# Product-key expert layer on Trainium2: tile order, row buffers, one-hot matrices and a scratch layout changed

## The chip, the cores and the metric

One core of one Trainium2 chip runs the whole program, two transformer blocks in one launch. The metric is the device time of one execution in microseconds (us). TensorE is PE here, VectorE DVE, ScalarE ACT, GpSimd POOL, and SyncE, which only issues DMAs, SP. All data is fp32; products that need full fp32 accuracy are made of three matmuls over a high and a low part of each operand (fp32r).

## The reference, cut to what matters

The change touches only the last stage, the expert layer at the end of the second block. For each of 512 tokens and 8 heads it finds the 16 best sums of two key scores out of 128 x 128 experts, and adds the outputs of these 128 experts, each one a vector of 1024 numbers in (`expert_down`) and one out (`expert_up`):

```python
v1, i1 = lax.top_k(sc[..., 0, :], PEER_TOPK)
v2, i2 = lax.top_k(sc[..., 1, :], PEER_TOPK)
cand = (v1[..., :, None] + v2[..., None, :]).reshape(b, s, PEER_HEADS, PEER_TOPK * PEER_TOPK)
cidx = (i1[..., :, None] * PEER_N_KEYS + i2[..., None, :]).reshape(b, s, PEER_HEADS, PEER_TOPK * PEER_TOPK)
top, pos = lax.top_k(cand, PEER_TOPK)
idx = jnp.take_along_axis(cidx, pos, axis=-1)
gate = jax.nn.softmax(top, axis=-1)
...
u = expert_down[ib]
act = jax.nn.gelu(jnp.einsum('bld,blhkd->blhk', hb, u), approximate=False)
coef = (gb * act.astype(F32)).astype(hb.dtype)
vv = expert_up[ib]
return jnp.einsum('blhk,blhkd->bld', coef, vv)
```

## The kernel before, in words

The 512 tokens are four tiles of 128. Tiles 0 to 2 (`DENSE` = 3) are computed densely: PE multiplies them with all 16384 experts, and a matrix G of gates, zero nearly everywhere, picks the chosen ones. Tile 3 is gathered: each of its tokens has its 128 rows of `expert_down` and then of `expert_up` fetched from HBM.

The stage (`peer_experts`, L2071) is a loop over 128 blocks. Each brings 1 MB of weights: `expert_down` in blocks 0 to 63, `expert_up` in blocks 64 to 127. SP loads them into a ring of three (L2145, L2150), ACT makes the high part (L2306, two halves), DVE the low part (L2355, two halves), PE multiplies (L264 to L266 in the first half, L2289 in the second). high and low have two buffers: ACT's high part of block q waits until PE has done block q-2, and DVE's low part waits for the high part.

Beside this stream every block carries small tasks, handed out at build time by `peer_plan` (L1907) from a budget per block. DVE does them in program order behind the two low parts of its block:

- `sel`: 24 pieces per tile that choose the experts (`Selection.piece`, L2003). Pieces 0 to 9 and 11 to 15 are maximum and index searches (L1991 to L1999), pieces 17, 18, 20 and 21 are tensor_tensor operations on 128x2048 elements (L2037, L2041). A tile's scores are loaded only after the tile before is done (L2156). `finish` makes its gates.
- `g`: a group of four tokens of a dense tile, 96 groups in all. DVE writes for each token two one-hot matrices of 128 x 128, eight tensor_scalar operations in all (L2376, L2378, the second one with the gate multiplied in); PE multiplies them into G of these tokens (`spread_group`, L2247, eight short matmuls), and ACT copies G out (L2330). Four buffers of one-hot matrices (`AB_RING`). SP stores G of 16 tokens to HBM (L2166, 24 stores of 1 MB) and loads it back by keys in the second half (L2178, one load of 1.5 MB for every four blocks).
- `dot`, `coef`, `acc`: the gathered tile. A row of 128x1024 (one expert for each token) is gathered by POOL with an indirect DMA (L2208) into a ring of eight buffers, DVE multiplies and sums it (L2384; 128 rows), and after `coef` 128 rows of `expert_up` are added into the result (L2395). Four of the eight buffers are the score and candidate buffers of the selection, so rows are gathered only once all four tiles are selected: dots begin in block 37.

POOL's program (L2214) is, block by block: in the second half the product of the dense activations (a_tile, gelu stored in the first half and loaded back, L2187) with G (L2221, tensor_tensor on 128x768), then the gathers whose buffer was freed in an earlier block. Behind the product come ACT's high part (L2346), DVE's low part (L2360) and PE.

The plan before, by blocks: 0 to 35 `sel`, with 2 or 3 groups each from block 12 on; 36 to 51 two groups, and three dots each from 37 on; 52 to 63 four dots each; 64 to 75 two or three dots; 77 to 119 two or three accs.

Of the kernel before, what the change touches and what calls it, by code (L numbers as in the profile page):

```python
# [23 lines left out]
P = 128  # L24
D = 1024
# [1864 lines left out]
ROW_RING = 8  # L1890
# [15 lines left out]

def peer_plan():  # L1907
# [9 lines left out]
    before = {"dot": ("sel", DENSE, last), "coef": ("dot", PEER_SLOTS - 1), "acc": ("coef", 0)}  # L1917
# [8 lines left out]

    for b in range(PEER_BLOCKS):
        budget, many = 5.5, 0
        if finish and placed_by(b - 2, ("sel", finish[0], last)):
            place(b, ("finish", finish.pop(0)))  # L1930
        while sel and budget > 0:
            i, n = sel[0]
            if i and n == 0 and not placed_by(b - 1, ("sel", i - 1, last)):
                break
            assert n < 11 or i == 0 or placed_by(b - 1, ("finish", i - 1))
            place(b, ("sel", *sel.pop(0)))
            budget -= SEL_COST[n]
# [7 lines left out]
        while rows and taken < (3 if many or b >= PAIRS else 4):  # L1945
# [10 lines left out]
class Selection:  # L1956
# [4 lines left out]
    def __init__(self, nc, io, st, sc, cand):  # L1961
# [14 lines left out]
        self.gates = st.sb("gates", [P, 2, PEER_SLOTS])  # L1976
        self.row_f = st.sb("row_f", [P, 2, PEER_SLOTS])
# [25 lines left out]
    def piece(self, i, n, turned):  # L2003
# [19 lines left out]
        elif n == 16:  # L2023
# [5 lines left out]
            else:  # L2029
                dve.wait_ge(turned, i)  # L2030
# [14 lines left out]
        else:  # L2045
            if i == DENSE:
# [11 lines left out]
    def finish(self, i, turned):  # L2058
        H, T, order, dve = PEER_HEADS, PEER_TOP, self.order, self.dve
        dve.wait_ge(self.exp_ready, i + 1)  # L2060
        if i >= 2:
            dve.wait_ge(turned, i - 1)
# [3 lines left out]
        order(dve.tensor_tensor(self.gates[:, i % 2, :].rearrange("p (h t) -> p h t", h=H), t,  # L2066
# [4 lines left out]
def peer_experts(nc, io, hn, hnT, h, ident, score_dram, a_dram, g_dram, out):  # L2071
# [12 lines left out]
    n_rows = 2 * PEER_SLOTS  # L2084
    with Stage(nc, "peer") as st:
# [23 lines left out]
        cand_rows = cand[:, :, :, :].rearrange("p h a b -> p (h a b)")  # L2109
        rows = [hn[:, 0, :], hn[:, 1, :], hn[:, 2, :], h[:, NT, :], sc[:, 0:D], sc[:, D:2 * D],  # L2110
                cand_rows[:, 0:D], cand_rows[:, D:2 * D]]
# [11 lines left out]
        idx_done, row_used, dots_gelu, coef_done = (  # L2123
            st.sem(x) for x in ("idx_done", "row_used", "dots_gelu", "coef_done"))
# [9 lines left out]
        with nc.Block() as block:  # L2134

            @block.sync
            def _(sp):
                sp.dma_start(select.iota[:, :], io["c_iota128"].partition_broadcast(P)).then_inc(select.iota_in, 16)
                sp.dma_start(sc[:, :], score_dram[0]).then_inc(select.sc_in, 16)
                for q in range(PEER_BLOCKS + 6):  # L2140
# [12 lines left out]
                    for i in range(1, NT):  # L2153
                        if at[("sel", i - 1, last_piece)] + 3 == q:
                            sp.wait_ge(select.selected, i)
                            sp.dma_start(sc[:, :], score_dram[i]).then_inc(select.sc_in, 16)  # L2156
# [5 lines left out]
                    for n in range(G_BATCHES):  # L2162
                        per = G_BATCH // G_TOK
                        if group_at[n * per + per - 1] + 4 == q:
                            sp.wait_ge(group_taken, (n + 1) * per)
                            sp.dma_start(g_dram[:, n, :, :].rearrange("p k t -> p (k t)"),  # L2166
                                         staged[:, n % 2, :, :].rearrange("p k t -> p (k t)")
                                         ).then_inc(staged_out[n % 2], 16)

                    for g in range(G_LOADS):  # L2170
                        if q == max(PAIRS - 1, PAIRS - 2 + 4 * g):
# [6 lines left out]
                            sp.dma_start(g_tile[:, g % 2, :, :, :], g_dram[:, :, g * G_KEYS:(g + 1) * G_KEYS, :]  # L2178
# [10 lines left out]
                sp.wait_ge(row_used, n_rows)  # L2189
                sp.dma_start(out[DENSE * P:NT * P, :], h[:, DENSE, :]).then_inc(stored, 16)  # L2190
# [6 lines left out]
            def _(pool):  # L2197
                def gather(n):
# [3 lines left out]
                    if n == 0:  # L2202
                        pool.wait_ge(select.selected, NT)
# [10 lines left out]
                for q in range(PEER_BLOCKS):  # L2214
                    b = q - PAIRS + 1
# [10 lines left out]
                    while done < n_rows and (row_at[done - ROW_RING] + 1 if done >= ROW_RING else  # L2226
                                             at[("sel", DENSE, last_piece)] + 1) <= q:
# [4 lines left out]
            def _(pe):  # L2232
                def turn(i):
                    pe.wait_ge(select.finished, i + 1)
                    if i >= 1:
                        pe.wait_ge(turn_taken, i)
                    for w, src in enumerate((select.picked[:, 0, :, :].rearrange("p h t -> p (h t)"),
                                             select.picked[:, 1, :, :].rearrange("p h t -> p (h t)"),
                                             select.gates[:, i % 2, :])):
# [11 lines left out]
                for q in range(PAIRS):  # L2251
                    tasks = [t for t in plan[q] if t[0] in ("finish", "g") and t[1] < DENSE]
# [4 lines left out]
                    for j in range(2):  # L2257
# [3 lines left out]
                        for k in range(KD):  # L2261
# [5 lines left out]
                            if k % 2 and tasks and not (j == 0 and k == 1):  # L2267
                                kind, i, *n = tasks.pop(0)
                                if kind == "finish":
                                    turn(i)  # L2270
# [27 lines left out]
            def _(act):  # L2298
                for q in range(PEER_BLOCKS + 2):
# [16 lines left out]
                    for task in (plan[q - 1] if 1 <= q <= PEER_BLOCKS else ()):  # L2316
                        if task[0] == "finish" and task[1] < DENSE:
                            i = task[1]
# [30 lines left out]
            def _(dve):  # L2349
                accumulated = 0  # L2350
                for q in range(PEER_BLOCKS):
# [10 lines left out]
                    for task in plan[q]:  # L2362
# [5 lines left out]
                        elif kind == "g":  # L2368
# [17 lines left out]
                        elif kind == "coef":  # L2386
                            dve.wait_ge(dots_gelu, 1)
                            dve.tensor_tensor(coef[:, :], dots[:, :], select.gates[:, DENSE % 2, :], ALU.mult
                                              ).then_inc(coef_done, 1)
                            dve.wait_ge(coef_done, 1)  # L2390
                        elif kind == "acc":
# [4 lines left out]
                                                     h[:, DENSE, :], ALU.mult, ALU.add).then_inc(row_used, 1)  # L2396
                for t in range(DENSE):
# [6 lines left out]
def second_block(nc, io, x, ident, out, dbg=None):  # L2404
# [4 lines left out]
    g_dram = nc.dram_tensor("scratch_g", [P, G_BATCHES, PEER_KEYS, G_BATCH], F32).ap()  # L2409
# [304 lines left out]
```

## Time and profile before

| | us |
|---|---|
| median of three runs | 5074.52 |
| lowest, highest | 5065.39, 5079.26 |
| the profiled execution | 5070.14 |
| its span, first to last instruction | 5068.4 |
| PE busy in it | 4175.7 (82%) |
| DVE busy | 3274.8 (65%) |
| ACT busy | 1977.1 (39%) |
| POOL busy | 620.0 (12%) |

The stage that is changed is the last quarter of the span, from 3735 us on. Busy times are sums over the whole program; what bounds this stage must be read in windows of it. Instructions of DVE overlap by some 0.1 us, so that the distance between two starts, not the duration, is what an instruction takes of the engine.

### The profile page before, as it was taken

To read this page: it belongs to the slowest core of one execution; us is meant where nothing else is said; L and a number is where in the kernel's file an instruction comes from. 1 tells how busy PE (TensorE), PEld (TensorE's weight loads), DVE (VectorE), ACT (ScalarE), POOL (GpSimd) and SP (SyncE) were. 2 spreads that over 40 slices of the span, in tenths; PEclk is the share of its full clock that TensorE was granted. 3 is DMA by queue.
4 is the path that set the end of the run, shared out by engine and by line. 5 is a ranking of instruction groups with operands and counts; after the bars stand their busy time and mean duration, and the time that the engine had idled before them with its cause. 6 is when DMAs were issued, how large, how long until landed. Compare 5 with 4: busy or idle time off the path is not lost. (4 is left out here: it accounts for less than half of the span.)

```text
span 5068.4 us, 60013 instructions
## 1 busy us (share of the span) xinstructions
PE 4175.7 (82%) x22904; PEld 3325.7 (66%) x22904; DVE 3274.8 (65%) x4709; ACT 1977.1 (39%) x2044; POOL 620.0 (12%) x391
## 2 busy tenths in 40 slices
PE   6674568999999999994946596778789889988889
PEld 6573355566556556553836576678679889966677
DVE  2335737888888888884275434423249999777776
ACT  2212206667676766663222122222223333322222
POOL 0000000000000000000000000000000014565774
PEclk8887679999999999997957767989889999999999
DMA  2020019999999999994211002122245559999996
GB/s 85 18 68 21 26 57 358 365 355 365 364 360 358 365 367 352 367 367 141 68 35 58 28 1 85 59 65 78 71 146 167 185 194 366 393 334 324 338 335 232
DMA packets 485002, 1054.27 MB, mean 208 GB/s; under 512 B 21634, under 2 KB 188290, under 8 KB 472392
## 3 DMA queue, kind: packets, MB, share of 16 engines
q1 hardware_dynamic: 444248, 908.46, 50.4%
q0 software_dynamic: 40560, 143.16, 7.9%
q8 instruction: 129, 2.11, 0.2%
q14 instruction: 65, 0.53, 0.0%
HBM read 986.23 MB, written 65.32 MB: 207 GB/s over the span
## 5 line engine op out<-in xcount | busy, mean ns | idle before, releaser
L1254 DVE TENSOR_TENSOR ffn_low<-ffn_raw,ffn_high 128x2048 fp32r<-128x2048 f32 (+1 forms) x576 | 1189.7, 2109 | 261.8 <-ACT ffn_high L1207 261.7
L1207 ACT CAST ffn_high<-ffn_raw 128x2048 fp32r<-128x2048 f32 (+1 forms) x576 | 986.9, 1765 | 418.2 <-DMA ffn_raw<-in_w_gate 145.7
L2306 ACT CAST peer_high<-peer_raw 128x1024 fp32r<-128x1024 f32 x256 | 256.3, 1049 | 542.8 <-PE peer_ps L266 294.1
L264 PE MATMUL peer_ps<-peerbuf_hnT_high,peer_high 128*128 128x384 f32 x1024 | 354.8, 347 | 21.4 <-ACT peer_high L2306 19.3
L2355 DVE TENSOR_TENSOR peer_low<-peer_raw,peer_high 128x1024 fp32r<-128x1024 f32 x256 | 311.1, 1256 | 93.1 <-ACT peer_high L2306 92.7
L265 PE MATMUL peer_ps<-peerbuf_hnT_high,peer_low 128*128 128x384 f32 x1024 | 346.0, 338 | 0.0
L266 PE MATMUL peer_ps<-peerbuf_hnT_low,peer_high 128*128 128x384 f32 x1024 | 345.9, 338 | 0.0
L2289 PE MATMUL peer_ps<-peer_high,peerbuf_hnT_high 128*128 128x512 f32 x768 | 249.7, 408 | 82.1 <-DVE peerbuf_hnT_low L2360 74.0
L264 PE MATMUL ffn_gate_p<-ffn_high,ffn_x_high 128*66 128x512 f32 (+1 forms) x768 | 290.0, 378 | 19.9 <-DVE ffn_low L1254 19.7
L264 PE MATMUL ffn_up_p<-ffn_high,ffn_x_high 128*66 128x512 f32 (+1 forms) x768 | 288.4, 376 | 7.2 <-DVE ffn_low L1254 7.2
L264 PE MATMUL ffn_down_p<-ffn_high,ffn_t_high 128*66 128x512 f32 x704 | 279.2, 397 | 15.8 <-DVE ffn_low L1254 15.8
L265 PE MATMUL ffn_gate_p<-ffn_high,ffn_x_low 128*66 128x512 f32 (+1 forms) x768 | 288.4, 375 | 0.0
L266 PE MATMUL ffn_gate_p<-ffn_low,ffn_x_high 128*66 128x512 f32 (+1 forms) x768 | 288.1, 375 | 0.0
L266 PE MATMUL ffn_up_p<-ffn_low,ffn_x_high 128*66 128x512 f32 (+1 forms) x768 | 287.9, 375 | 0.0
L265 PE MATMUL ffn_up_p<-ffn_high,ffn_x_low 128*66 128x512 f32 (+1 forms) x768 | 287.8, 375 | 0.0
L265 PE MATMUL ffn_down_p<-ffn_high,ffn_t_low 128*66 128x512 f32 x704 | 277.3, 394 | 0.0
L266 PE MATMUL ffn_down_p<-ffn_low,ffn_t_high 128*66 128x512 f32 x704 | 276.7, 393 | 0.0
L2289 PE MATMUL peer_ps<-peer_low,peerbuf_hnT_high 128*128 128x512 f32 x768 | 245.0, 401 | 0.0
L2289 PE MATMUL peer_ps<-peer_high,peerbuf_hnT_low 128*128 128x512 f32 x768 | 244.0, 400 | 0.0
L2289 PEld LDWEIGHTS peer_ps<-peer_high,peerbuf_hnT_high 128*128 128x128 f32 x768 | 149.4, 197 | 120.5 <-ACT peer_high L2306 76.1
L2204 POOL CAST peer_row_idx<-peer_row_f 128x256 uint32<-128x256 f32 x1 | 0.4, 398 | 1826.3 <-DVEq L2051 1826.3
L264 PEld LDWEIGHTS peer_ps<-peerbuf_hnT_high,peer_high 128*128 128x128 f32 x1024 | 195.6, 191 | 21.9 <-ACT peer_high L2306 19.4
(558 smaller groups left out, 9683.5 us busy)
## 6 DMA issues: line engine op xcount, KB each, us to landing
ffn_raw<-in_w_gate SPq DMA_DIRECT2D x80, 2048.0 KB, 9.6
ffn_raw<-in_w_up SPq DMA_DIRECT2D x80, 2048.0 KB, 9.9
ffn_raw<-in_w_down SPq DMA_DIRECT2D x80, 2048.0 KB, 10.7
peer_raw<-in_peer_down_t SPq DMA_DIRECT2D x64, 1024.0 KB, 6.8
peer_raw<-in_peer_up_t SPq DMA_DIRECT2D x64, 1024.0 KB, 8.6
scratch_a<-peer_gelu SPq DMA_DIRECT2D x64, 384.0 KB, 7.7
scratch_g<-peer_spread SPq DMA_DIRECT2D x24, 1024.0 KB, 9.7
peer_spread<-scratch_g SPq DMA_DIRECT2D x16, 1536.0 KB, 19.0
```

The costliest lines, as they stand in the source:

```text
L264: pe.matmul(out, hi_l, hi_r, start=start, stop=False)
L265: pe.matmul(out, lo_l, hi_r, start=False, stop=False)
L266: return pe.matmul(out, hi_l, lo_r, start=False, stop=stop)
L1207: act.copy(half_of(high, q, h), half_of(raw, q, h)).then_inc(high_done, 1)
L1254: dve.tensor_tensor(half_of(low, q, h), half_of(raw, q, h), half_of(high, q, h).bitcast(F32), ALU.subtract).then_inc(low_done, 1)
L2204: pool.tensor_copy(row_idx[:, :, :], select.row_f[:, :, :]).then_inc(idx_done, 1)
L2289: last = pe.matmul(ps[:, 2 * t + half, :], lhs, right[:, q % 2, cols], start=(b == 0 and j == 0 and c == 0 and right is high), stop=(b == ...
L2306: act.copy(high[:, q % 2, cols], raw[:, q % PR_RAW, cols]).then_inc(high_done, 1)
L2355: dve.tensor_tensor(low[:, q % 2, cols], raw[:, q % PR_RAW, cols], high[:, q % 2, cols].bitcast(F32), ALU.subtract).then_inc(low_done, 1)
```

## The change

- The gathered tile is selected first (`SEL_TILES`), its gates have a buffer of their own, and its dots may start once its `finish` is placed. The row ring has seven buffers in place of eight: the three dense tiles of `hn`, the spare tile of `h`, and the three dense tiles of `h`, which are stored to HBM at the start of the stage and loaded back before the final addition.
- A group's one-hot matrices are made by two tensor_tensor operations on 128x512 (is_equal of the broadcast iota and the broadcast keys of four tokens). The gate is multiplied in by POOL, a tensor_tensor on 128x512 for each group, in program order ahead of the gathers of the same block; PE waits for it.
- The plan: a budget of 6.0 for `sel` (5.5 before), up to three groups per block also after the selection; one dot per block while `sel` is there, then four per block up to block 63, and 2, 2 or 3 accs per block in the second half. Worked out with the new rules: blocks 0 to 20 `sel` alone, one dot each from 12 on; blocks 21 to 34 `sel` with 36 groups and 14 dots; blocks 35 to 54 three groups and four dots each; blocks 55 to 61 25 dots; accs in 63 to 117. Blocks 8, 17 and 26 hold only the last, short piece of a tile's selection, beside at most one group and one dot.
- G in HBM is laid out by loads: a store of 1 MB now goes out in pieces of 512 bytes, and a load of 1.5 MB reads one run of 12288 bytes per partition. Before it was the other way round.

```diff
-ROW_RING = 8
+ROW_RING = 7
+SEL_TILES = [DENSE] + list(range(DENSE))
@@ peer_plan
-    before = {"dot": ("sel", DENSE, last), "coef": ("dot", PEER_SLOTS - 1), "acc": ("coef", 0)}
+    before = {"dot": ("finish", 0), "coef": ("dot", PEER_SLOTS - 1), "acc": ("coef", 0)}
+    def group_ready(b):
+        return groups and placed_by(b - 2, ("finish", groups[0][0] + 1))
-        budget, many = 5.5, 0
+        budget, many = 6.0, 0
-            if groups and many < 3 and placed_by(b - 2, ("finish", groups[0][0])):
+            if group_ready(b) and many < 3:
-        while not sel and groups and many < 2 and placed_by(b - 2, ("finish", groups[0][0])):
+        while not sel and group_ready(b) and many < 3:
-        while rows and taken < (3 if many or b >= PAIRS else 4):
+        most = 1 if sel else 4 if b < PAIRS else 2 + (b % 3 == 0)
+        while rows and taken < most:
@@ peer_experts
-        rows = [hn[:, 0, :], hn[:, 1, :], hn[:, 2, :], h[:, NT, :], sc[:, 0:D], sc[:, D:2 * D],
-                cand_rows[:, 0:D], cand_rows[:, D:2 * D]]
+        rows = [hn[:, i, :] for i in range(DENSE)] + [h[:, NT, :]] + [h[:, i, :] for i in range(DENSE)]
@@ sync
+                sp.dma_start(h_dram.rearrange("t p d -> p t d"), h[:, 0:DENSE, :]).then_inc(h_out, 16)
-                            sp.dma_start(g_dram[:, n, :, :].rearrange("p k t -> p (k t)"),
-                                         staged[:, n % 2, :, :].rearrange("p k t -> p (k t)")
+                            sp.dma_start(g_dram[:, :, n, :].rearrange("g p c -> p g c"),
+                                         staged[:, n % 2, :, :].rearrange("p (g k) t -> p g (k t)", g=G_LOADS)
-                            sp.dma_start(g_tile[:, g % 2, :, :, :], g_dram[:, :, g * G_KEYS:(g + 1) * G_KEYS, :]
+                            sp.dma_start(g_tile[:, g % 2, :, :, :].rearrange("p n k t -> p n (k t)"), g_dram[g]
                 sp.wait_ge(row_used, n_rows)
+                sp.dma_start(h[:, 0:DENSE, :], h_dram.rearrange("t p d -> p t d")).then_inc(h_back, 16)
@@ gpsimd
                     if n >= ROW_RING:
                         pool.wait_ge(row_used, n - ROW_RING + 1)
+                    elif n == DENSE + 1:
+                        pool.wait_ge(h_out, 16)
...
                 for q in range(PEER_BLOCKS):
+                    for task in plan[q]:
+                        if task[0] == "g":
+                            i, n = task[1], group_no[task]
+                            gate = turned[:, i % 2, 2, task[2] * G_TOK:(task[2] + 1) * G_TOK]
+                            pool.wait_ge(onehot_done, 2 * n + 2)
+                            pool.tensor_tensor(onehot[:, n % AB_RING, 1, :, :], onehot[:, n % AB_RING, 1, :, :],
+                                               gate.unsqueeze(2).broadcast_to([P, G_TOK, PEER_KEYS]),
+                                               ALU.mult).then_inc(gated, 1)
...
                     while done < n_rows and (row_at[done - ROW_RING] + 1 if done >= ROW_RING else
-                                             at[("sel", DENSE, last_piece)] + 1) <= q:
+                                             rows_chosen + 1) <= q:
                         gather(done)
@@ tensor, spread_group
-                    pe.wait_ge(onehot_done, 2 * G_TOK * (n + 1))
+                    pe.wait_ge(onehot_done, 2 * n + 2)
+                    pe.wait_ge(gated, n + 1)
@@ vector
-                            for t in range(G_TOK):
-                                col = task[2] * G_TOK + t
-                                first, second, gate = (turned[:, i % 2, w, col:col + 1] for w in range(3))
-                                dve.tensor_scalar(onehot[:, n % AB_RING, 0, t, :], select.iota[:, :], first, None,
+                            for w in range(2):
+                                key = turned[:, i % 2, w, task[2] * G_TOK:(task[2] + 1) * G_TOK]
+                                dve.tensor_tensor(onehot[:, n % AB_RING, w, :, :],
+                                                  select.iota[:, :].unsqueeze(1).broadcast_to([P, G_TOK, PEER_KEYS]),
+                                                  key.unsqueeze(2).broadcast_to([P, G_TOK, PEER_KEYS]),
                                                   ALU.is_equal).then_inc(onehot_done, 1)
-                                dve.tensor_scalar(onehot[:, n % AB_RING, 1, t, :], select.iota[:, :], second, gate,
-                                                  ALU.is_equal, ALU.mult).then_inc(onehot_done, 1)
+                dve.wait_ge(h_back, 16)
                 for t in range(DENSE):
                     dve.wait_ge(tile_summed, t + 1)
@@ second_block
-    g_dram = nc.dram_tensor("scratch_g", [P, G_BATCHES, PEER_KEYS, G_BATCH], F32).ap()
+    g_dram = nc.dram_tensor("scratch_g", [G_LOADS, P, G_BATCHES, G_KEYS * G_BATCH], F32).ap()
```

## Rows read from the trace of the kernel before

**Rows 1.** Windows that begin at DVE's low part of blocks 0, 21, 35, 55, 64, 127

```profile
core 0: us, PE busy (x) PEld busy (x) DVE busy (x) ACT busy (x) POOL busy (x), PEclk, DMA share, GB/s
3745.90:3962.20 216.30, 200.06 (x1168) 196.17 (x1168) 210.76 (x755) 79.73 (x115) 0.00 (x0) 0.97 0.54 173
3962.20:4145.40 183.20, 157.80 (x977) 151.98 (x977) 181.85 (x631) 63.70 (x97) 0.00 (x0) 0.99 0.53 171
4145.40:4344.70 199.30, 197.88 (x1232) 197.56 (x1233) 182.44 (x445) 77.70 (x117) 88.09 (x65) 0.99 0.94 354
4344.70:4421.80 77.10, 74.92 (x433) 74.63 (x432) 63.16 (x90) 24.85 (x37) 39.16 (x30) 1.00 1.03 404
4421.80:5048.90 627.10, 545.02 (x2281) 443.88 (x2280) 461.85 (x389) 178.30 (x196) 395.10 (x227) 0.93 0.91 321
```

**Rows 2.** Waits of 4421.8 to 5048.9, total us, times, longest us

```profile
POOL peer_spread L2221 <- DMA peer_spread<-scratch_a: 202.9, 27, 19.4
```

**Rows 3.** Timeline of SP around one load of G

```profile
4706.43 0.54 SPq L2178 DMA_DIRECT2D peer_spread<-scratch_g  x1
4707.06 12.91 SPq L2187 DMA_DIRECT2D peer_spread<-scratch_a  x1
4720.02 0.43 SPq L2150 DMA_DIRECT2D peer_raw<-in_peer_up_t  x1
```

**Rows 4.** Windows: blocks 42-49, 54-60, second half, load of G, just after, no accs

```profile
4216.70:4297.70 81.00, 81.00 (x514) 81.00 (x513) 75.33 (x193) 31.58 (x49) 33.32 (x25) 1.00 0.96 352
4336.40:4394.60 58.20, 58.20 (x338) 58.20 (x337) 48.99 (x70) 19.33 (x29) 37.21 (x29) 1.00 1.02 415
4635.00:4800.00 165.00, 139.20 (x582) 113.46 (x581) 124.14 (x97) 45.15 (x49) 111.70 (x65) 0.92 0.96 335
4714.00:4717.00 3.00, 3.00 (x15) 2.49 (x14) 2.90 (x4) 0.90 (x1) 2.69 (x2) 1.00 1.11 304
4725.00:4728.00 3.00, 0.00 (x0) 0.00 (x0) 0.00 (x0) 0.00 (x0) 1.61 (x1) 0.83 1.02 402
5008.10:5040.70 32.60, 32.60 (x145) 26.99 (x144) 19.49 (x13) 10.92 (x13) 10.37 (x4) 1.00 0.44 151
```

**Rows 5.** Timeline of DVE in block 39: start, us of one, instruction

```profile
4187.51 1.22 DVE L2355 TENSOR_TENSOR peer_low<-peer_raw,peer_high 128x1024 fp32r<-128x1024 f32 x1
4188.65 0.28 DVE L2376 TENSOR_SCALAR peer_spread<-peer_iota,peer_turned 128x128 f32<-128x128 f32 x1
4188.84 0.34 DVE L2378 TENSOR_SCALAR peer_spread<-peer_iota,peer_turned 128x128 f32<-128x128 f32 x1
...
4190.46 0.28 DVE L2376 TENSOR_SCALAR peer_spread<-peer_iota,peer_turned 128x128 f32<-128x128 f32 x1
...
4193.41 1.23 DVE L2384 SCALAR_TENSOR_TENSOR peer_cand<-peer_cand,peerbuf_hn 128x1024 f32<-128x1024 f32 x1
...
4194.56 1.23 DVE L2384 SCALAR_TENSOR_TENSOR peerbuf_hn<-peerbuf_hn 128x1024 f32<-128x1024 f32 x1
```

**Rows 6.** Timeline of DVE at the end of a tile's selection, and its next piece

```profile
3809.68 2.29 DVE L2037 TENSOR_TENSOR peer_sc<-peer_partf,peer_iota 128x2048 f32<-128x2048 f32 x1
...
3819.36 0.23 DVE L2055 COPY peer_top<-peer_shift 128x128 f32<-128x128 f32 x1
3819.74 2.36 DVE L2355 TENSOR_TENSOR peer_low<-peer_raw,peer_high 128x1024 fp32r<-128x1024 f32 x2
3824.47 1.65 DVE L1991 MAX8 peer_v<-peer_sc 128x8 f32<-128x128 f32 x8 [2.38 <-DMA peer_sc<-scratch_score]
```

**Rows 7.** POOL's product: alone, beside DVE, and DVE's dots at that time

```profile
4686.16 1.80 POOL L2221 TENSOR_TENSOR peer_spread<-peer_spread 128x768 f32<-128x768 f32 x1 [11.40 <-DMA peer_spread<-scratch_a]
4498.23 2.01 POOL L2221 TENSOR_TENSOR peer_spread<-peer_spread 128x768 f32<-128x768 f32 x1
4497.33 1.21 DVE L2384 SCALAR_TENSOR_TENSOR peerbuf_hn<-peerbuf_hn 128x1024 f32<-128x1024 f32 x1
4498.47 2.85 DVE L2384 SCALAR_TENSOR_TENSOR peerbuf_hn<-peerbuf_hn 128x1024 f32<-128x1024 f32 x1
4501.26 2.35 DVE L2355 TENSOR_TENSOR peer_low<-peer_raw,peer_high 128x1024 fp32r<-128x1024 f32 x2
```

**Rows 8.** Gathers: the first two of the stage (median us to landing), then all 256

```profile
peerbuf_hn<-in_peer_down,peer_row_idx POOLq DMA_INDIRECT x2, 4.9
DMA to landing us min/median/max: 4.5/8.7/19.1
```

**Rows 9.** Timeline of SP at the start of the stage

```profile
3735.73 0.42 SPq L2139 DMA_DIRECT2D peer_sc<-scratch_score  x1
3736.20 12.39 SPq L2145 DMA_DIRECT2D peer_raw<-in_peer_down_t  x4
```

More of the change, by code:

```diff
@@ L1976, in __init__ @@
         self.gates = st.sb("gates", [P, 2, PEER_SLOTS])
+        self.row_gates = st.sb("row_gates", [P, PEER_SLOTS])
         self.row_f = st.sb("row_f", [P, 2, PEER_SLOTS])
@@ L2028, in piece @@
                 dve.wait_ge(self.iota_in, 16)
-            else:
-                dve.wait_ge(turned, i)
+            elif i >= 2:
+                dve.wait_ge(turned, i - 1)
         elif n < 23:
@@ L2045, in piece @@
         else:
-            if i == DENSE:
+            if i == 0:
                 for a, b in ((0, 1), (1, 0)):
@@ L2060, in finish @@
         dve.wait_ge(self.exp_ready, i + 1)
-        if i >= 2:
-            dve.wait_ge(turned, i - 1)
+        gates = self.row_gates[:, :] if i == 0 else self.gates[:, i % 2, :]
+        if i >= 3:
+            dve.wait_ge(turned, i - 2)
         t = self.top[:, i % 2, :, :]
@@ L2065, in finish, with peer_experts @@
         order(dve.reciprocal(self.total[:, :], self.total[:, :]))
-        order(dve.tensor_tensor(self.gates[:, i % 2, :].rearrange("p (h t) -> p h t", h=H), t,
+        order(dve.tensor_tensor(gates.rearrange("p (h t) -> p h t", h=H), t,
                                 self.total[:, :].unsqueeze(2).broadcast_to([P, H, T]), ALU.mult))
         dve.sem_inc(self.finished, 1)
-def peer_experts(nc, io, hn, hnT, h, ident, score_dram, a_dram, g_dram, out):
+def peer_experts(nc, io, hn, hnT, h, ident, score_dram, a_dram, g_dram, h_dram, out):
     plan, at = peer_plan()
@@ L2084, in peer_experts @@
     n_rows = 2 * PEER_SLOTS
+    rows_chosen = at[("sel", 0, last_piece)]
     with Stage(nc, "peer") as st:
@@ L2122, in peer_experts @@
             st.sem(x) for x in ("product_done", "c_high_done", "c_low_done", "tile_summed", "added", "stored"))
-        idx_done, row_used, dots_gelu, coef_done = (
-            st.sem(x) for x in ("idx_done", "row_used", "dots_gelu", "coef_done"))
+        idx_done, row_used, dots_gelu, coef_done, h_out, h_back, gated = (
+            st.sem(x) for x in ("idx_done", "row_used", "dots_gelu", "coef_done", "h_out", "h_back", "gated"))
         row_in = [st.sem(f"row_in{s}") for s in range(ROW_RING)]
@@ L2233, in turn @@
                 def turn(i):
-                    pe.wait_ge(select.finished, i + 1)
+                    pe.wait_ge(select.finished, i + 2)
                     if i >= 1:
@@ L2251, in _ @@
                 for q in range(PAIRS):
-                    tasks = [t for t in plan[q] if t[0] in ("finish", "g") and t[1] < DENSE]
+                    tasks = [t for t in plan[q] if t[0] == "g" or (t[0] == "finish" and t[1] >= 1)]
                     pe.wait_ge(high_done, 2 * (q + 1))
@@ L2269, in _ @@
                                 if kind == "finish":
-                                    turn(i)
+                                    turn(i - 1)
                                 else:
@@ L2316, in _ @@
                     for task in (plan[q - 1] if 1 <= q <= PEER_BLOCKS else ()):
-                        if task[0] == "finish" and task[1] < DENSE:
-                            i = task[1]
+                        if task[0] == "finish" and task[1] >= 1:
+                            i = task[1] - 1
                             act.wait_ge(turn_done, 3 * (i + 1))
@@ L2387, in _ @@
                             dve.wait_ge(dots_gelu, 1)
-                            dve.tensor_tensor(coef[:, :], dots[:, :], select.gates[:, DENSE % 2, :], ALU.mult
+                            dve.tensor_tensor(coef[:, :], dots[:, :], select.row_gates[:, :], ALU.mult
                                               ).then_inc(coef_done, 1)
@@ L2617, in second_block @@
                 peer_scores(nc, io, qT, score_dram)
-            peer_experts(nc, io, hn, hnT, x, ident, score_dram, a_dram, g_dram, out)
+            peer_experts(nc, io, hn, hnT, x, ident, score_dram, a_dram, g_dram, hd_dram, out)
 def two_blocks(nc, io, out):
```

10 lines of the change are left out of this document (5 added, 5 removed).

## The prediction, made blind

> **What bounds the kernel now.** Only the stage from 3735 us on is changed, so I read its windows first, cut where the plan, old or new, changes its mix [rows 1]. Between blocks 0 and 34 DVE is busy 211 of 216 us and 182 of 183 us: DVE bounds it, while DMA is half idle. Blocks 35 to 54 take 199.3 us with PE busy 198: PE bounds, but DVE (182) and DMA (0.94) are close behind. Of these, blocks with two groups and three dots take 81.0 / 8 = 10.12 us, and blocks without groups 58.2 / 7 = 8.31 us [rows 4]; PE therefore pays 0.90 us per group and 8.31 for the dense product. In the second half 63 blocks take 627.1 us, 9.95 each, though PE alone needs 32.6 / 4 = 8.15 [rows 1, 4]. The missing 113 us are a wait of the data: POOL's product waits 202.9 us for a_tile [rows 2], and SP shows why. Behind the load of G in pieces of 512 bytes the next DMA takes 12.91 us to issue [rows 3]. While the pieces are moved the DMA engines are full at 304 GB/s, where right after they are full at 402 [rows 4].
>
> **One-hot matrices.** A group takes DVE 1.81 us (4188.65 to 4190.46), a low part of 1024 elements 1.14, a dot 1.15 [rows 5]; a tensor_tensor with the same kind of broadcast operands on 2048 elements takes 2.33 [rows 6]. So 512 elements are about 0.6, and a new group 1.2: 0.6 us less of DVE, 59 us over 96 groups.
>
> **The gate on POOL.** POOL's product of 768 elements lasts 1.80 us alone; 512 are 1.20 by proportion. It is not free for DVE: the dot that starts at 4498.47, beside the product of 4498.23, holds DVE for 2.79 us (to 4501.26) where its neighbour took 1.14 [rows 7]. The POOL instruction of 1.80 us held DVE up for 1.64, nearly its whole length. In proportion a gate product costs DVE 1.09 whenever DVE's next operations read two operands from SBUF, as the new one-hot operations, the dots and the low parts do. That is more than the 0.6 saved. Beside a search piece of the selection I take it as free; the trace has no POOL product beside one, so the bounds are 0 and 1.09. The Trainium skill (SBUF — State Buffer, Who interferes with whom) says that a DVE instruction with two SBUF inputs and a GpSimd instruction that reads SBUF exclude each other for the whole instruction. By that a gate product would cost the full 1.20, and the sum would be some 9 us higher; the trace agrees but for the 0.16 us.
>
> **The ring of seven with four dots per block.** In a block q with dots n to n+3, row n+3 uses the buffer of row n-4, freed in block q-1. The loop on POOL issues its gather in block q, and there behind the three gate products, which wait for DVE's groups of block q. With eight buffers the four rows of a block were all issued a block earlier. Time after the third group: dot 1 runs (1.15), then the third gate product holds DVE (1.09), at about 2.3 the gather of row n+3 is issued, dots 2 and 3 end at 4.6, and dot 4 waits for the landing. A gather takes 4.9 us from issue to landing on an idle system and 8.7 in the median of all 256, most of them with DMA over 90% busy [rows 8]. The new blocks move more bytes in more time, about two thirds of what DMA can: I take 6, nearer to the idle value. Dot 4 then starts at 8.3 and DVE idles 3.7 us per block, with bounds of 2.6 and 6.4. Low parts of the next block stand behind it on DVE, and PE behind these.
>
> **The sum, stretch by stretch**, against [rows 1]:
> - Start: SP stores 1.5 MB of h between the scores and the first weights, and the weights queue behind it [rows 9]. At 402 GB/s that is 4 us: +4. The reload at the end is issued when the last a_tile has gone, under PE's last blocks: 0.
> - Blocks 0 to 20 (216.3): 24 groups leave, 24 x 1.81 = -43; nine dots come, +10; one search piece more, +2. Blocks 8 and 17 have 3 and 4 us of DVE work where PE needs 8.3, which gives back 9, also because the next tile's scores are loaded only after the last piece [rows 6]. -22.
> - Blocks 21 to 34 (183.2): 37 old groups -67, 36 new ones +43, 14 dots +16, later pieces +3, short block 26 +3, and gate products on half of the groups (those followed by a dot, a low part or a tensor_tensor piece) 18 x 1.09 = +20. +18.
> - Blocks 35 to 54 (199.3): two low parts 2.3, three groups 3.6, three gate products 3.3, four dots 4.6, together 13.8 us of DVE against 8.31 + 3 x 0.90 = 11.0 of PE; with the wait of 3.7, 17.5. Twenty blocks: 350, +151.
> - Blocks 55 to 63 (77.1): PE bound at 8.3 both times. 0.
> - Blocks 64 to 126 (627.1): the gathers fall from three to 2.33 per block. A block moves 1.05 MB of weights, 0.39 of a_tile, 0.39 of G and 1.22 of rows, 3.05 MB; at the 335 GB/s of this stretch with its DMA share of 0.96 taken to 1, i.e. 350, that is 8.7 us, at 402 it is 7.6, and PE needs 8.15. With G in long runs the stall behind its load should go, and fewer rows leave DVE more room. I take 8.45: 532, -95; bounds -113 (PE alone) and -76 (8.75).
>
> Sum +4 - 22 + 18 + 151 + 0 - 95 = +56, on the profiled execution's 5070.14: **5126 us**. That execution lies 4 us under the median of three runs, inside their scatter. 0.3% (15 us) is about what a measurement of this kernel can tell from no change.
>
> **Rivals.**
> 1. *The gathers come in time*: a row is asked for earlier than I read from POOL's program, and dot 4 finds it there. Then blocks 35 to 54 cost DVE's 13.8, 74 us less: 5052, faster. It decides once a gather is issued 2.6 us (4.9 less 2.3) ahead of where I put it. For it: DMA is half idle in such blocks, so nothing but the order holds a gather back. Against it: that order, and the minimum of 4.5 us [rows 8], which still leaves a wait of 2.2. A half-way case (POOL's third product gets in ahead of dot 1, and gathers take 4.5, so that dot 4 waits 1.1) gives 20 x 2.6 = 52 less, 5074, no change.
> 2. *POOL's product does not hold DVE, and gathers are in time*: broadcast operands or a shorter operation may behave otherwise than the product of 768. Blocks 35 to 54 fall to PE's 11.0, 220 us, and the second stretch loses its 20: 5126 - 130 - 20 = 4976. Against it stands the dot of 2.79 us [rows 7].
> 3. *The layout of G brings nothing*: the 5 us stall after each of 16 loads comes from the 1.5 MB and the gathers together, not from the pieces, and remains. Then the second half is 16 x (4 x 8.15 + 5) = 602 less one block's 8, 594: -33 in place of -95, 5188. The Trainium skill (DMA: Bandwidth & Descriptors, Specifications) gives 512 bytes as enough for line rate, by which this rival would be right. The trace speaks against it: 304 GB/s with pieces, 402 without, both with the DMA engines full [rows 4].
> 4. *Gathers take 8.7 us*, the median of before [rows 8], because the stores of G, now in pieces of 512 bytes, crowd the queues in just these blocks: 20 x 2.7 = 54 more, 5180. Against it: more time per block than before for the bytes.
>
> **How the numbers follow.** Forecast 0.58, with its own range 5085 to 5160; rival 1 0.13, its half-way case 0.07, rival 2 0.08, rivals 3 and 4 0.07 each. The range of 8 in 10 takes in the forecast, rival 1 and the dearer rivals, and leaves out rival 2: 5045 to 5190. Faster by over 0.3%: rivals 1 and 2, 0.21. Slower: the forecast and rivals 3 and 4, less 0.02 for the low end of the forecast, 0.70. Within 0.3%: the half-way case and that, 0.09.
>
> **What would show it.** Right: blocks 35 to 54 some 17 us apart, with DVE idle before the fourth dot until a gather lands, dots or one-hot operations of some 1.7 to 2.3 us beside gate products of 1.2, PE waiting for DVE's low part; blocks 0 to 20 some 20 us shorter; in the second half no issue of 12.9 us on SP, little wait of the product for a_tile, blocks near 8.4. Wrong: blocks 35 to 54 at 11 to 14 us, or DVE instructions of unchanged length beside the gate products, or a second half that stays near 600 us.

## The result, and the profile after

The changed kernel takes 5099.12 us in the median of six runs (5097.06 to 5107.88), the kernel before 5074.1 (5065.39 to 5079.26): ratio 1.0056, 95% interval 1.0043 to 1.0069. It is slower, as forecast, by 25 us in place of the 52 between 5126 and 5074.

The profiled execution (5107.88 us, span 5106.1) is one of the longer ones. Its stage begins at 3746.2 us with SP's first issue, 10.9 us later than before (3735.3), in code that the change doesn't touch; over the ten profiles of this study (those of the kernels below among them) that start scatters from 3726 to 3750. So I compare the stage by itself, from that first issue to the end: 5068.4 - 3735.3 = 1333.1 us before, 5106.1 - 3746.2 = 1359.9 after. These +26.8 us are what the 25 us between the medians come from.

Windows of the changed kernel, cut at the same blocks as [rows 1] (0, 21, 35, 55, 64, 127):

```profile
core 0: us, PE busy (x) PEld busy (x) DVE busy (x) ACT busy (x) POOL busy (x), PEclk, DMA share, GB/s
3761.20:3953.40 192.20, 179.59 (x1001) 176.69 (x1002) 179.86 (x589) 66.12 (x92) 20.64 (x16) 0.97 0.61 212
3953.40:4150.10 196.70, 161.68 (x942) 153.86 (x941) 191.65 (x430) 62.41 (x95) 79.97 (x49) 0.94 0.58 186
4150.10:4475.80 325.70, 258.87 (x1475) 249.30 (x1475) 263.63 (x328) 95.54 (x147) 188.43 (x140) 0.91 0.83 260
4475.80:4559.50 83.70, 72.09 (x392) 71.83 (x393) 55.98 (x74) 22.24 (x34) 43.02 (x30) 0.92 1.00 388
4559.50:5086.60 527.10, 518.13 (x2280) 427.65 (x2279) 432.82 (x315) 177.09 (x195) 323.72 (x184) 1.00 0.89 340
```

Against [rows 1] that makes -24.1, +13.5, +126.4, +6.6 and -100.0 us; the start (first issue to the first low part) is 15.0 in place of 10.6, +4.4. Sum +26.8. Two large moves of opposite sign stand behind half a per cent.

The third line has the loss. DVE is busy 264 of 326 us, PE 259: neither is full, so something waits. One block of it, block 44, on the timeline of DVE (start, us, instruction, idle time before it and what ended it) shows what:

```profile
4295.72 2.36 DVE L2376 TENSOR_TENSOR peer_low<-peer_raw,peer_high 128x1024 fp32r<-128x1024 f32 x2
4297.99 5.39 DVE L2396 TENSOR_TENSOR peer_spread<-peer_iota,peer_turned 128x512 f32<-128x512 f32 x6
4303.30 1.21 DVE L2404 SCALAR_TENSOR_TENSOR top_h<-top_h,peerbuf_hn 128x1024 f32<-128x1024 f32 x1
...
4304.44 2.05 DVE L2404 SCALAR_TENSOR_TENSOR top_h<-top_h,peerbuf_hn 128x1024 f32<-128x1024 f32 x1
...
4306.42 1.21 DVE L2404 SCALAR_TENSOR_TENSOR top_h<-top_h,peerbuf_hn 128x1024 f32<-128x1024 f32 x1
...
4310.76 1.23 DVE L2404 SCALAR_TENSOR_TENSOR top_h<-top_h,peerbuf_hn 128x1024 f32<-128x1024 f32 x1 [3.12 <-DMA top_h<-in_peer_down,peer_row_idx]
...
4311.91 1.22 DVE L2376 TENSOR_TENSOR peer_low<-peer_raw,peer_high 128x1024 fp32r<-128x1024 f32 x1
```

and the timeline of POOL in the same block:

```profile
4299.36 1.42 POOL L2232 TENSOR_TENSOR peer_spread<-peer_spread,peer_turned 128x512 f32<-128x512 f32 x1 [4.53 <-DVE peer_spread L2396]
4301.40 1.42 POOL L2232 TENSOR_TENSOR peer_spread<-peer_spread,peer_turned 128x512 f32<-128x512 f32 x1 [0.63 <-DVE peer_spread L2396]
4303.45 1.95 POOL L2232 TENSOR_TENSOR peer_spread<-peer_spread,peer_turned 128x512 f32<-128x512 f32 x1 [0.63 <-DVE peer_spread L2396]
4305.56 1.77 POOL L2220 DMA_INDIRECT top_h<-in_peer_down,peer_row_idx  x1 [0.15 <-issue]
```

Read from top to bottom: two low parts (2.27 us), six one-hot operations that take 5.31 us (4297.99 to 4303.30), a dot, a second dot of 2.05 us beside POOL's third product, a third dot, then 3.12 us of nothing until a row lands that POOL asked for at 4305.56, behind its three products. The block is 4311.91 - 4295.72 = 16.2 us. This is the picture that the prediction drew, with smaller numbers.

That block is no exception. The waits of DVE in this stretch, total us, times, longest us, are all waits for rows:

```profile
DVE top_h L2404 <- DMA top_h<-in_peer_down,peer_row_idx: 36.2, 11, 4.7
DVE peerbuf_hn L2404 <- DMA peerbuf_hn<-in_peer_down,peer_row_idx: 25.4, 8, 3.6
```

They are 61.6 us in 19 waits; with DVE's 263.6 busy they make 325.2 of the 325.7 us. PE's granted clock is lower here than before (0.91 against 0.99 in [rows 1]), but that leaves no time over for it to explain.

### The profile page after: what moved, and what is told of

Same layout as the page of the kernel before. It is cut to its first block and busy times, and to the rows that moved or that the text cites. A ratio compares the mean times of both kernels' runs of the same rounds, so it can differ in the third digit from the quotient of the medians.

```text
span 5106.1 us, 59541 instructions
## 1 busy us (share of the span) xinstructions
PE 4201.8 (82%) x22904; PEld 3345.9 (66%) x22904; DVE 3299.1 (65%) x4133; ACT 1976.0 (39%) x2044; POOL 754.0 (15%) x487
## 5 line engine op out<-in xcount | busy, mean ns | idle before, releaser
L264 PE MATMUL peer_ps<-peerbuf_hnT_high,peer_high 128*128 128x384 f32 x1024 | 369.0, 360 | 108.3 <-issue 54.0
L2376 DVE TENSOR_TENSOR peer_low<-peer_raw,peer_high 128x1024 fp32r<-128x1024 f32 x256 | 338.0, 1361 | 116.1 <-ACT peer_high L2327 115.7
L265 PE MATMUL peer_ps<-peerbuf_hnT_high,peer_low 128*128 128x384 f32 x1024 | 356.4, 348 | 0.0
L266 PE MATMUL peer_ps<-peerbuf_hnT_low,peer_high 128*128 128x384 f32 x1024 | 356.3, 348 | 0.0
L2310 PE MATMUL peer_ps<-peer_high,peerbuf_hnT_high 128*128 128x512 f32 x768 | 238.1, 391 | 9.0 <-DVE peerbuf_hnT_low L2381 5.2
L1101 POOL DMA_INDIRECT scratch_h<-ffn_result,ffn_y_rows x16 | 44.7, 2795 | 1352.4 <-DVE ffn_result L1246 1239.5
## 6 DMA issues: line engine op xcount, KB each, us to landing
ffn_raw<-in_w_down SPq DMA_DIRECT2D x80, 2048.0 KB, 10.6
```

The costliest lines, as they stand in the source:

```text
L264: pe.matmul(out, hi_l, hi_r, start=start, stop=False)
L265: pe.matmul(out, lo_l, hi_r, start=False, stop=False)
L266: return pe.matmul(out, hi_l, lo_r, start=False, stop=stop)
L2310: last = pe.matmul(ps[:, 2 * t + half, :], lhs, right[:, q % 2, cols], start=(b == 0 and j == 0 and c == 0 and right is high), stop=(b == ...
L2376: dve.tensor_tensor(low[:, q % 2, cols], raw[:, q % PR_RAW, cols], high[:, q % 2, cols].bitcast(F32), ALU.subtract).then_inc(low_done, 1)
```

## The experiments

All times of stretches below are windows of each kernel's own profile, cut at its low parts of blocks 0, 21, 35, 55, 64 and 127. Ratios are to the kernel before, which took 5074.84 us beside the first four variants and 5074.99 beside the last four.

### POOL's gathers ahead of the gate products

```diff
                 for q in range(PEER_BLOCKS):
+                    if q < PAIRS - 1:
+                        while done < n_rows and (row_at[done - ROW_RING] + 1 if done >= ROW_RING else
+                                                 rows_chosen + 1) <= q:
+                            gather(done)
+                            done += 1
                     for task in plan[q]:
                         if task[0] == "g":
```

> The changed kernel, with POOL's gathers of a block issued ahead of its gate products in the first half; nothing else moves. Theory A (the order on POOL makes the fourth row late): in blocks 35 to 54 the wait of 3.1 us before the fourth dot goes, and a block falls from 16.3 us to DVE's own sum, 2.3 low parts + 3.7 groups + 2.5 hold by the gate products + 4.6 dots = 13.1; 20 blocks give 64 us back, 5099 becomes about 5035, under the kernel before. Rival B (the blocks are bound by something the order does not touch: stores of G in 512 byte pieces, PE waiting for gated groups, ACT waiting for PE): the wait before the dot shrinks but the block stays near 16 us and the time within 15 us of 5099.

5041.62 us, ratio to before 0.9935 (0.9919 to 0.9952): 57.5 us off the changed kernel, for an edit of the order of instructions alone. Theory A holds. The window of blocks 35 to 54:

```profile
4146.60:4416.80 270.20, 241.02 (x1471) 221.37 (x1470) 269.66 (x328) 93.69 (x146) 221.42 (x140) 1.00 0.94 313
```

DVE is now busy 269.7 of 270.2 us: the whole wait is gone, and 13.5 us per block are DVE's own (13.1 expected). The stretches before it are as they were to 1.1 us; blocks 55 to 63 take 81.0 (83.7), the second half 532.7 (527.1).

### The gate multiplied in on DVE again

```diff
-                            for w in range(2):
-                                key = turned[:, i % 2, w, task[2] * G_TOK:(task[2] + 1) * G_TOK]
-                                dve.tensor_tensor(onehot[:, n % AB_RING, w, :, :],
...
+                            for t in range(G_TOK):
+                                col = task[2] * G_TOK + t
+                                first, second, gate = (turned[:, i % 2, w, col:col + 1] for w in range(3))
+                                dve.tensor_scalar(onehot[:, n % AB_RING, 0, t, :], select.iota[:, :], first, None,
                                                   ALU.is_equal).then_inc(onehot_done, 1)
+                                dve.tensor_scalar(onehot[:, n % AB_RING, 1, t, :], select.iota[:, :], second, gate,
+                                                  ALU.is_equal, ALU.mult).then_inc(onehot_done, 1)
@@
-                            pool.tensor_tensor(onehot[:, n % AB_RING, 1, :, :], onehot[:, n % AB_RING, 1, :, :],
-                                               gate.unsqueeze(2).broadcast_to([P, G_TOK, PEER_KEYS]),
-                                               ALU.mult).then_inc(gated, 1)
```

> The changed kernel, with the one-hot matrices made as before by eight tensor_scalar operations that take the gate in, and no product on POOL. Theory A (both the hold and the order come from the gate product on POOL): a group costs DVE 1.81 in place of 1.22 + 0.83 of hold, and POOL reaches the gathers at once, so no row is late. Blocks 35 to 54: 2.3 + 5.4 + 4.6 = 12.3 us, 246 in place of 326; blocks 21 to 34 within 10 us of the 197 of the changed kernel. About 5020. Rival B (other causes bind these blocks): 16 us per block stay, 5099. Rival C (one-hot work itself is the cost, and the new form a gain that only the row wait hides): slower than e1_gathers_first by some 10 us.

5024.04 us, ratio 0.9903 (0.9879 to 0.9927). Windows of blocks 21 to 34 and 35 to 54:

```profile
3943.10:4147.10 204.00, 162.01 (x952) 152.60 (x950) 199.27 (x646) 62.35 (x95) 22.84 (x14) 0.96 0.56 182
4147.10:4395.60 248.50, 230.82 (x1456) 227.06 (x1455) 247.72 (x688) 92.58 (x145) 128.23 (x79) 0.97 0.98 340
```

Blocks 35 to 54 are 12.4 us each and again all DVE. The one-hot matrices "made faster" cost more here than the old ones: 270 us with them and with the gathers in order, 248 without. In blocks 21 to 34, where half of the gate products run beside searches by the prediction's count, the new form wins, 196.7 to 204.0. Rival C has its sign wrong: this kernel is 17.6 us faster than the one with POOL's gathers first, not slower.

### The product left out, the wait for it kept

```diff
                             pool.wait_ge(onehot_done, 2 * n + 2)
-                            pool.tensor_tensor(onehot[:, n % AB_RING, 1, :, :], onehot[:, n % AB_RING, 1, :, :],
-                                               gate.unsqueeze(2).broadcast_to([P, G_TOK, PEER_KEYS]),
-                                               ALU.mult).then_inc(gated, 1)
+                            pool.sem_inc(gated, 1)
```

> The changed kernel, with the gate product on POOL left out but POOL's wait for DVE's groups kept (G then holds ones in place of gates). Theory A: the hold of 2.5 us per block goes, six one-hot operations take 3.7 us in place of 5.3; the order stays, so the gather for the fourth row is issued just after the third group: dots 1 to 3 take 3.45 us, the gather 5.2, so that dot 4 still waits about 1.8. Block 10.6 + 1.8 = 12.4 us, 248 for blocks 35 to 54. If the product does not hold DVE (rival), the one-hot operations keep their length of 5.3 us for six, or the block changes by less than 1 us.

One execution, 5040.79 us; this kernel leaves the gates out of G. From the timeline of DVE, a group of six and the fourth dot of the same block:

```profile
4228.02 3.69 DVE L2393 TENSOR_TENSOR peer_spread<-peer_iota,peer_turned 128x512 f32<-128x512 f32 x6
...
4238.89 1.23 DVE L2401 SCALAR_TENSOR_TENSOR top_h<-top_h,peerbuf_hn 128x1024 f32<-128x1024 f32 x1 [3.74 <-DMA top_h<-in_peer_down,peer_row_idx]
```

The six operations take 3.62 us (4228.02 to the next start, 4231.64) in place of 5.31: two products hold DVE 0.85 us each, and the second dot is back at 1.15 from 1.98, the third 0.83. That is the price of the product, seen by taking it away. Blocks 21 to 34 take 183.3 us in place of 196.7: there the 36 products cost 13.4 us in all. The trace of the changed kernel shows where: beside a product ten low parts of these blocks last 2.05 us in place of 1.21 and six one-hot operations 1.41 in place of 0.68, 12.8 us together, while the searches keep their length (the maximum search on 128x256, MAX8, takes 0.41 us with a product beside it and without). This is the case that the prediction had no row for: beside a search the product is free.

The wait was mis-sized: 3.74 us in this block where I expected 1.8, and 284.9 us for the stretch in place of 248. The gather needs 6.4 us from issue to landing here. A store of G is under way (SP 4228.98, landed 4239.82), and the DMA engines are full while the dot waits (share 1.12 from 4235.4 to 4238.9). Blocks 40 and 44, in which no store of G is issued, take 12.3 and 12.4 us with waits of 1.8 and 1.9, just as expected; the other six of the blocks 40 to 47 issue one and take 14.3 to 15.3. So the wait depends on the latency as the prediction said, and the latency goes with what else DMA carries. In the changed kernel the gather is issued 3 us later in its block, with a store further along, and the landing takes 5.0 to 5.7 us in blocks 40 to 47: without the product the order on POOL costs more, 72 us of waits in place of 62.

### Three dots in blocks with groups

```diff
-        most = 1 if sel else 4 if b < PAIRS else 2 + (b % 3 == 0)
+        most = 1 if sel else (3 if many else 4) if b < PAIRS else 2 + (b % 3 == 0)
```

> The changed kernel, with three dots in place of four in blocks that have groups (the order on POOL kept, ring of seven). Theory A: with three dots each row of a block is asked for a block earlier, so no dot waits: 2.3 + 3.7 + 2.5 + 3.4 = 11.9 us per block in 35 to 54, 238 in place of 326; some dots move behind block 64 and accs end by block 124. About 5020. Rival B (stores of G and the load of DMA bind): fewer gathers help in proportion only, 326 x 4/5 at best 290, and dots still wait.

5028.26 us, ratio 0.9907 (0.989 to 0.9923). Its window of blocks 35 to 54:

```profile
4154.50:4394.10 239.60, 230.91 (x1459) 220.12 (x1459) 239.06 (x286) 93.49 (x145) 192.30 (x118) 1.00 0.94 307
```

Eighteen of the twenty blocks take 11.8 or 11.9 us, as expected to 0.1 us, and DVE is busy all the time; 10 us are given back in blocks 55 to 63 (93.7), where some of the dots that were left over are done. A ring of seven serves three rows per block without a wait, with the same late order on POOL. Rival B's 290 is excluded.

### The layout of G alone, and undone

On the kernel before, only these three edits; on the changed kernel, only these three taken back.

```diff
-                            sp.dma_start(g_dram[:, n, :, :].rearrange("p k t -> p (k t)"),
-                                         staged[:, n % 2, :, :].rearrange("p k t -> p (k t)")
+                            sp.dma_start(g_dram[:, :, n, :].rearrange("g p c -> p g c"),
+                                         staged[:, n % 2, :, :].rearrange("p (g k) t -> p g (k t)", g=G_LOADS)
-                            sp.dma_start(g_tile[:, g % 2, :, :, :], g_dram[:, :, g * G_KEYS:(g + 1) * G_KEYS, :]
+                            sp.dma_start(g_tile[:, g % 2, :, :, :].rearrange("p n k t -> p n (k t)"), g_dram[g]
-    g_dram = nc.dram_tensor("scratch_g", [P, G_BATCHES, PEER_KEYS, G_BATCH], F32).ap()
+    g_dram = nc.dram_tensor("scratch_g", [G_LOADS, P, G_BATCHES, G_KEYS * G_BATCH], F32).ap()
```

> The kernel before with the new layout of G in HBM alone (stores of 1 MB in pieces of 512 bytes, loads in long runs); plan, one-hot matrices, ring as before. Theory L (the pieces of the load are what stalls the second half): SP's issue of 12.9 us behind the load goes, blocks with three accs take the 8.5 us that DVE needs, the second half falls from 627 to some 545 to 560, the first half is unchanged: 5074 less 70 to 80, about 5000. Theory W (fewer gathers per block are what helps, and the layout little): the second half stays over 600, about 5060.

> The changed kernel with the layout of G of before. Theory L: the stall of 5 us or more after each of the 16 loads of G comes back, the second half goes from 527 to 590 to 605 us: 5165 to 5180. Theory W (2.33 gathers per block in place of three give the gain): second half within 20 us of 527, 5099 to 5120. In blocks 35 to 54 the stores of G are in runs of 8 KB again: if the pieces delay the gathers, the wait before the fourth dot shrinks from 3.1 us by up to 1 us, 20 us less.

Alone 5025.91 us, ratio 0.9914 (0.9897 to 0.993); undone 5133.44, ratio 1.0115 (1.0098 to 1.0132). The second half, with both kernels of the case, as a square:

| blocks 64 to 126, us | layout of before | new layout |
|---|---|---|
| plan of before, three accs per block | 627.1 | 586.1 |
| new plan, 2, 2 or 3 accs per block | 563.9 | 527.1 |

The right-hand value of the first row and the left-hand one of the second are these windows:

```profile
4413.70:4999.80 586.10, 535.61 (x2259) 434.52 (x2258) 480.26 (x391) 176.25 (x192) 387.67 (x227) 0.96 0.89 341
4553.30:5117.20 563.90, 529.81 (x2280) 432.89 (x2279) 428.08 (x314) 176.39 (x194) 312.63 (x185) 0.98 0.91 320
```

The layout is worth 41 and 37 us, the plan 63 and 59. The plan means fewer gathers per block, but also 35 dots that the old plan leaves to blocks 64 to 75; the blocks of the accs, 77 to 119, alone fall from 412 to 358 us in the new layout, so most of it is there. Neither theory holds alone; the two effects add, and the larger one is the plan's, where I had expected 70 to 80 us from the layout. SP around a load of G, layout alone:

```profile
4632.57 0.47 SPq L2178 DMA_DIRECT2D peer_spread<-scratch_g  x1
4633.14 0.38 SPq L2187 DMA_DIRECT2D peer_spread<-scratch_a  x1
```

and the same on the changed kernel with the old layout:

```profile
4804.12 0.54 SPq L2187 DMA_DIRECT2D peer_spread<-scratch_g  x1
4804.75 8.38 SPq L2196 DMA_DIRECT2D peer_spread<-scratch_a  x1
```

The issue stall belongs to the pieces: 12.91 us in [rows 3], 8.38 in the new plan with its fewer gathers, 0.38 with long runs. But POOL's product still waits 166.6 us for a_tile in the layout-alone kernel ([rows 2]: 202.9), and 172.7 us in the changed kernel, whose second half is 100 us shorter. So the sum of that wait doesn't tell what the stretch loses. What follows the time better is how long ACT waits behind that product for the high part: 208.7 us before, 125.5 with the layout alone, 114.0 with the plan alone, 57.2 with both. Blocks 35 to 54 are 325.5 us with the old layout and 325.7 with the new, and 199.3 and 199.4 in the old plan: stores in pieces of 512 bytes delay neither plan more than stores of 8 KB do. They do take more of DMA: its share is 0.83 against 0.79, and 0.99 against 0.94.

### Two versions from what was learned

The changed kernel with no product on POOL, one tensor_tensor for the first one-hot matrix and four tensor_scalar with the gate for the second, three dots in blocks with groups, the store of h behind the first two weight loads:

```diff
+                            key = turned[:, i % 2, 0, task[2] * G_TOK:(task[2] + 1) * G_TOK]
+                            dve.tensor_tensor(onehot[:, n % AB_RING, 0, :, :],
+                                              select.iota[:, :].unsqueeze(1).broadcast_to([P, G_TOK, PEER_KEYS]),
+                                              key.unsqueeze(2).broadcast_to([P, G_TOK, PEER_KEYS]),
+                                              ALU.is_equal).then_inc(onehot_done, 1)
+                            for t in range(G_TOK):
+                                col = task[2] * G_TOK + t
+                                second, gate = (turned[:, i % 2, w, col:col + 1] for w in (1, 2))
+                                dve.tensor_scalar(onehot[:, n % AB_RING, 1, t, :], select.iota[:, :], second, gate,
+                                                  ALU.is_equal, ALU.mult).then_inc(onehot_done, 1)
```

> The changed kernel with: no product on POOL; the first one-hot matrix by one tensor_tensor for four tokens (0.61), the second by four tensor_scalar with the gate (1.04); three dots in blocks with groups; the store of h behind the first weights. A group takes DVE 1.65, a block of 35 to 54 2.3 + 4.95 + 3.4 = 10.7 us, under PE's 11.0, so PE bounds them: 221 us. The start falls by 4.5 us to 10.5, blocks 21 to 34 are near 198, 55 to 63 near 94, the second half near 526. Stage 1262 in place of 1360: about 5000.

The kernel before with the new layout and the same one-hot matrices:

> The kernel before with the new layout of G and the mixed one-hot matrices (one tensor_tensor, four tensor_scalar with the gate). If theory L holds, e5_layout_alone less 0.16 us for each of the 61 groups in blocks that DVE bounds, 10 us: about 4990, the lowest. If the reordering of the changed kernel is worth more than it costs, e7_combined is lower than this one.

4994.31 us, ratio 0.9849 (0.9832 to 0.9865), and 5021.79, ratio 0.9905 (0.9889 to 0.9922). The first is faster than both kernels of the case, by 81 us (before) and 105 (changed). Its windows of blocks 35 to 54, 55 to 63 and 64 to 126:

```profile
4133.00:4348.50 215.50, 215.45 (x1405) 215.06 (x1404) 213.57 (x468) 90.28 (x140) 96.06 (x60) 1.00 1.00 346
4348.50:4438.70 90.20, 84.78 (x498) 84.46 (x496) 63.50 (x89) 32.05 (x47) 44.38 (x36) 0.99 1.03 407
4438.70:4965.30 526.60, 511.44 (x2238) 420.57 (x2239) 446.03 (x339) 172.17 (x187) 332.66 (x197) 0.99 0.93 350
```

PE and DVE are both full in the first line: the two bounds have met at 10.8 us. The start, from SP's first issue to the first low part, is 11.5 us, so the store of h ahead of the weights cost 3.6 of its 15.0. The parts of this kernel were not run one by one. The second kernel came out 32 us slower than forecast, with the layout-alone kernel 26 us over its own; the 4 us between these two lie inside their scatter, so what the mixed one-hot matrices bring by themselves on the old plan is not shown. Both keep three gathers per block in the second half (580.3 and 586.1 us), and that is what my 545 to 560 left out. With the same layout and the same one-hot matrices the reordered kernel is 27 us ahead of the old order: the reordering of the change is worth having, its fourth dot per block and its gate product were not.

## Why the prediction was right

Direction and range were right, and so was the mechanism of the large loss; the middle was 27 us too slow. By its own steps, forecast against measured on the changed kernel, in us:

| step | forecast | measured |
|---|---|---|
| start, store of h ahead of the weights | +4 | +4.4 |
| blocks 0 to 20 | -22 | -24.1 |
| blocks 21 to 34 | +18 | +13.5 |
| blocks 35 to 54 | +151 | +126.4 |
| blocks 55 to 63 | 0 | +6.6 |
| blocks 64 to 126 | -95 | -100.0 |
| sum | +56 | +26.8 |

- *One-hot matrices*: six operations in 3.62 us without the product, 0.60 each: as worked out from the longer shapes.
- *The gate on POOL*: right in kind, mis-sized. The shortest product on 128x512 lasts 1.04 us, not the 1.20 that I scaled from 768 elements, and holds DVE 0.83 to 0.85, not 1.09. DVE was to be busy 13.8 us per block, 276 in the stretch, and is busy 263.6: 12 us of the 25 by which this stretch was too dear. In blocks 21 to 34 the products cost 13.4 us where I had put 20; that they are free beside searches held. The Trainium skill (SBUF — State Buffer, Who interferes with whom) has the two exclude each other for the whole instruction; the runs agree in kind, and about 0.2 us of POOL's 1.04 does not cost DVE anything.
- *The ring of seven*: right, and shown by two edits that each remove the wait, the order on POOL and the number of dots. I forecast 3.7 us of wait; block 44 has 3.1, and the stretch 61.6 in place of 74, the other 12 of the 25. The issue was placed right, 2.3 us after the third group (4303.30 to 4305.56); the gather lands after 5.2 us, not 6, and the dots before it are done 0.3 us sooner than forecast.
- *Blocks 55 to 63*: the 0 failed. The plan puts one block of 15.4 us there (block 58), in which ACT waits up to 14.8 us for a store of gelu outputs to land (the waits of 4490 to 4520), with the DMA share at 1.00. Full engines alone don't explain it: the same blocks of the same plan take 75.3 us with the gate on DVE, at a share of 1.03, and 81.0 with POOL's gathers first. The cause stays open.
- *Blocks 64 to 126*: the number was right, 8.37 us per block against 8.45, the reasons only in part. I took 8.45 between PE's 8.15 and 8.75 by bytes; PE is busy 518 of the 527 us, at a DMA share of 0.89, so PE bounds it, and that the choice fell so close is luck. The reading that the 113 us missing before are the wait for a_tile behind the load of G gave too much to the layout: of the 100 us, it has about 40, and the changed kernel still has 172.7 us of that wait.
- *Rivals*: 1 and 2 fall with the 3.12 us wait and the 2.05 us dot. 3 falls with 41 and 37 us; the Trainium skill (DMA: Bandwidth & Descriptors, Specifications) gives 512 bytes as enough for line rate, and this trace does not agree: with loads in such pieces the second half moves 320 GB/s at a DMA share of 0.91, with long runs 340 at 0.89, and the pieces stall SP's issue besides. 4 falls as stated: the median of all gathers fell to 6.5 us, and the stores' pieces change nothing in the time of blocks 35 to 54.

## What to carry to other kernels

An instruction moved to POOL is not off DVE's hands when both read two operands from SBUF: here it cost DVE 0.84 us of its 1.04 in such places, so price it at nearly its whole length, and look where DVE works on searches instead (here the form with the product won there, 196.7 to 204.0 us). Every operation added to a queue also stands ahead of what that queue does next: here a product in front of gathers, with a ring one row too small for the burst, cost DVE 62 us of waits where the products themselves cost it 51 (263.6 us busy, 212.3 without them), and moving one loop up by a few lines took the waits back. A ring of eight in the changed kernel was not run. When two stretches move by 100 us in opposite directions, test each part on the old kernel alone, and take it alone out of the new one; here that showed which part to keep. A total of waits is no price: POOL waited 166.6 us in a stretch of 586 and 172.7 in one of 527.

## What the runs showed that I had not expected

POOL's tensor_tensor on 128x512 takes 1.04 us at least where 128x768 takes 1.80 [rows 7]: 0.58 of the time for 0.67 of the elements. The two differ in their operands too (the gate is broadcast in the first), so this need not be size alone. And a gather that takes 5.2 us in block 44 of the changed kernel takes 6.4 in the kernel without the product, where it is issued earlier: the first runs at a DMA share of 0.51 (4305.6 to 4310.8), the second beside a store of G, with the engines full. Taking work away from POOL moved the gather into the store.
